# A decoder step on one core: another order of the steps in the front's projections and gates

## The reference, cut to what matters

```
xn   = rms_norm(x, g_attn)
proj = xn @ w_in      # columns: 512 pooling, 384 query latent, 256 kv latent, 32 rope, 2 x 1024 gates
q    = rms_norm(rope(rms_norm(q_lat) @ w_uq), head gains)     # 8 heads x 96
c_kv = rms_norm(c_kv);  k_r = rope(k_r)
k    = rms_norm([c_kv @ w_uk, k_r])                           # 8 heads x 96
d    = trailing means of u_pool over 2, 4, 8, 16 rows - u_pool
pool_out = (d @ w_pool_map) * pool_scale
gated    = (sigmoid(gate 0) * pool_out, sigmoid(gate 1))
```

## Time and profile before

| what | value |
|---|---|
| median of three runs | 2182.67 us (2181.5 to 2183.23) |
| profiled execution | 2183.03 us |
| its span | 2181.1 us |
| mean granted clock of TensorE | 0.979 |
| busy in the span | PE 2081.8, PEld 1915.4, DVE 1177.9, ACT 816.8, POOL 384.4 us |
| front ends on TensorE | 447.5 us; the attention's first product starts at 464.5 us |

### The profile page before, as it was taken

How to read it: one execution, slowest core, us unless ns; L and a number is a source line. 1 busy time by engine, 2 the same in 40 slices (tenths; PEclk the granted TensorE clock), 3 DMA queues, 4 the chain that set the end, 5 groups by cost and what they waited for, 6 DMA issues and landing times. The chain is left out here.

```text
span 2181.1 us, 35232 instructions
## 1 busy us (share of the span) xinstructions
PE 2081.8 (95%) x12669; PEld 1915.4 (88%) x12669; DVE 1177.9 (54%) x2356; ACT 816.8 (37%) x1589; POOL 384.4 (18%) x441
## 2 busy tenths in 40 slices
PE   6998999969988999999999989999999999999998
PEld 5887999968877999999999968899998989999997
DVE  3764311137765777677767744544444444444444
ACT  4553111136653566566656642422111112212111
POOL 1110000024441145355535420000000000000000
PEclk8999999989998999999999989999999999999999
DMA  4223222125422312222222134011111111111102
GB/s 153 86 74 96 60 80 80 66 80 152 127 73 64 88 36 64 72 67 66 63 71 66 34 119 175 22 57 58 39 58 38 38 38 40 57 38 58 38 19 87
DMA packets 146190, 152.69 MB, mean 70 GB/s; under 512 B 50694, under 2 KB 122102, under 8 KB 145021
## 3 DMA queue, kind: packets, MB, share of 16 engines
q1 hardware_dynamic: 140325, 128.28, 20.0%
q0 software_dynamic: 5728, 22.65, 3.3%
HBM read 124.77 MB, written 25.97 MB: 69 GB/s over the span
## 5 line engine op out<-in xcount | busy, mean ns | idle before, releaser
L104 PE MATMUL ps<-mh,f_w1h 128*128 128x384 f32 (+1 forms) x768 | 250.6, 326 | 0.0
L106 PE MATMUL ps<-mh,f_w1l 128*128 128x384 f32 (+1 forms) x768 | 250.5, 326 | 0.0
L105 PE MATMUL ps<-ml,f_w1h 128*128 128x384 f32 (+1 forms) x768 | 250.3, 326 | 0.0
L1920 ACT ACTIVATE tail_room<-ps 128x384 f32<-128x384 f32 (+1 forms) x96 | 45.5, 474 | 502.1 <-PE ps L106 502.1
L1373 ACT ACTIVATE sq<-ps 128x512 f32<-128x512 f32 x256 | 153.2, 598 | 207.6 <-PE ps L106 207.5
L1965 DVE TENSOR_TENSOR t_m<-t_m,ps 128x512 f32<-128x512 f32 x256 | 171.7, 685 | 106.9 <-PE ps L106 106.9
L105 PE MATMUL ps<-f_late_l,f_late_h 128*128 128x512 f32 x512 | 199.9, 390 | 0.0
L106 PE MATMUL ps<-f_late_h,f_late_l 128*128 128x512 f32 x512 | 199.8, 390 | 0.0
L104 PE MATMUL ps<-f_late_h 128*128 128x512 f32 x512 | 199.3, 389 | 0.0
L1945 DVE TENSOR_TENSOR tail_room<-tail_room 128x384 f32<-128x384 f32 (+1 forms) x96 | 51.5, 536 | 253.7 <-ACT tail_room L1920 253.7
L104 PE MATMUL ps<-wq,cTh 128*128 128x320 f32 x512 | 171.9, 336 | 2.4 <-DVE g_attn_b L1453 1.5
(11 more groups left out here) (350 smaller groups left out, 5045.9 us busy)
## 6 DMA issues: line engine op xcount, KB each, us to landing
f_raw<-in_w_ff SPq DMA_DIRECT2D x32, 1024.0 KB, 5.4
c_ring<-in_cache_kv_latent SPq DMA_DIRECT2D x192, 128.0 KB, 2.0
m_raw<-in_w_in SPq DMA_DIRECT2D x20, 512.0 KB, 3.9
gated<-gate POOLq DMA_DIRECT2D x8, 1088.0 KB, 5.1
pa_gm<-gated SPq DMA_DIRECT2D x16, 512.0 KB, 5.3
c_early<-in_cache_kv_latent SPq DMA_DIRECT2D x64, 128.0 KB, 2.1
fr_x<-in_x_prompt SPq DMA_DIRECT2D x8, 512.0 KB, 3.5
mixed<-pa_mixed SPq DMA_DIRECT2D x16, 256.0 KB, 2.2
```

The costliest lines, as they stand in the source:

```text
L104: nc.tensor.matmul(out, lh, rh, start=first, stop=False)
L105: nc.tensor.matmul(out, lh, rl, start=False, stop=False)
L106: return nc.tensor.matmul(out, ll, rh, start=False, stop=last)
L1920: nc.scalar.activation(z[:, a, 0:w], ps[:, 2 * par + a, 0:w], ACT.Relu).then_inc(S["relu"], 1)
```

## The change

The loop is taken apart into one function a step and engine, and these are called in a new order. No computation is added or dropped, and all instructions keep their shapes, but for where they stand and for the bank that one tile uses.

- Tile 1's latents go to banks 4 and 5 and follow tile 0's at once. The transposes of x of tile 1 stand between chunks 5 and 6 of tile 0's latents. For that SP loads x of tile 1 behind the fifth weight chunk and x of tile 2 ahead of `w_uq` and `w_uk`; ScalarE and VectorE handle x of tile 1 between weight chunks 4 and 5, and its high and low parts between chunks 6 and 7.
- Within a tile's latents all of bank 3 (288 columns) comes first, then the wait for `ctc`, then bank 2 (384 columns).
- ScalarE copies queries and keys of tile 7 inside step 8. The splits of chunks 0 to 3 are spread among the last tiles' steps.
- Heads of tile 7 follow project(0), heads of tile 8 follow project(1), the earlier state's transposes follow project(2), the tail's follow project(4).
- VectorE splits chunks 4 and 5 behind the first and second window, chunks 2 and 3 before all windows.
- The pooled products are issued as (j, 2), (j + 1, 0) after project(6 + 2j) and (j + 1, 1) after project(7 + 2j). VectorE splits chunk 7 + 2j before it scales (j, 2).

```diff
+        lat_bank = lambda i: 4 if i == 1 else 2
 # sync
-            for i, (pieces, *_rest) in enumerate(tiles):
-                wait_past(sp, s["xnd"], i - 1)
...
-                if i == 0:
-                    for k in range(KD):
...
+            load_x(0)
+            for k in range(KD):
+                wait_past(sp, wl_done, k - WR + 1)
+                sp.dma_start(wraw[k % WR], w_lat[:, k, :]).then_inc(w_in[k % WR], 16)
+                if k == WR - 1:
+                    load_x(1)
+            load_x(2)
+            sp.dma_start(w_uq[:], A["w_uq"].rearrange("(k p) n -> p k n", p=P)).then_inc(uq_in, 16)
+            sp.dma_start(w_uk, A["w_uk"].rearrange("(k p) h d -> p k (h d)", p=P)).then_inc(uq_in, 16)
+            for i in range(3, N):
+                load_x(i)
 # scalar
+            square_x(0)
+            copy_x(0)
+            for k in range(WR):
+                split_lat(k)
+            square_x(1)
+            split_lat(5)
+            split_lat(6)
+            copy_x(1)
+            split_lat(7)
+            copy_lat(0)
+            square_lat(0)
...
+            root_lat(0)
+            square_x(2)
+            copy_lat(1)
+            copy_turned(0)
+            copy_x(2)
+            square_lat(1)
+            root_lat(1)
+            copy_turned(1)
+            for g in range(2, N):
...
+                if g == N - 1:
+                    copy_qk(N - 2)
+                copy_q(g - 2, 1)
+            split_chunk(0)
+            square_qk(N - 2)
+            copy_qk(N - 1)
+            split_chunk(1)
+            square_qk(N - 1)
+            copy_q(N - 2, 0)
+            copy_q(N - 2, 1)
+            copy_channels(0)
+            split_chunk(2)
+            copy_q(N - 1, 0)
+            copy_q(N - 1, 1)
+            copy_channels(1)
+            split_chunk(3)
 # vector
+            mean_x(0)
+            scale_x(0)
+            low_x(0)
+            for k in range(WR):
+                low_lat(k)
+            mean_x(1)
+            scale_x(1)
+            low_lat(5)
+            low_lat(6)
+            low_x(1)
+            low_lat(7)
+            mean_lat(0)
+            scale_lat(0)
...
+            mean_x(2)
+            scale_x(2)
...
             dve.wait_ge(s["qkp"], N)
-            for c in range(2, 6):
-                split_chunk(c)
-                g = c - 2
+            for g in range(4):
...
+                if g < 2:
+                    split_chunk(4 + g)
                 for b, (lo, hi) in enumerate(groups):
                     i = 3 * j + b
+                    if b == 2 and 7 + 2 * j < NCH:
+                        split_chunk(7 + 2 * j)
...
-                if 7 + 2 * j < NCH:
-                    split_chunk(7 + 2 * j)
 # tensor
+            def latents(i):
+                pe.wait_ge(s["xtl"], 2 * i + 2)
+                if i >= 2:
+                    pe.wait_ge(s["latc"], 2 * i)
+                for k in range(KD):
+                    latent(i, k, 1)
+                if i >= 2:
+                    pe.wait_ge(s["ctc"], i)
+                for k in range(KD):
+                    last = latent(i, k, 0)
+                last.then_inc(s["latp"], 1)
+            turn_x(0)
+            pe.wait_ge(s["xtl"], 2)
+            for k in range(KD):
+                if k == 6:
+                    turn_x(1)
+                pe.wait_ge(wl_done, k + 1)
+                latent(0, k, 0)
+                last = latent(0, k, 1)
+            last.then_inc(s["latp"], 1)
+            latents(1)
+            turn_latents(0)
+            turn_x(2)
+            queries_and_keys(0)
+            turn_latents(1)
+            for g in range(2, N):
+                latents(g)
+                if g + 1 < N:
+                    turn_x(g + 1)
+                queries_and_keys(g - 1)
+                turn_heads(g - 2, 0)
+                turn_latents(g)
+                turn_heads(g - 2, 1)
+            queries_and_keys(N - 1)
+            project(0)
+            turn_heads(N - 2, 0)
+            turn_heads(N - 2, 1)
+            project(1)
+            turn_heads(N - 1, 0)
+            turn_heads(N - 1, 1)
+            project(2)
...
+            project(3)
+            project(4)
...
+            project(5)
...
-            for j in range(KD):
-                pooled(j)
-                if j + 1 < KD:
-                    project(6 + 2 * j)
-                    project(7 + 2 * j)
+            pooled(0, 0)
+            pooled(0, 1)
+            for j in range(KD - 1):
+                project(6 + 2 * j)
+                pooled(j, 2)
+                pooled(j + 1, 0)
+                project(7 + 2 * j)
+                pooled(j + 1, 1)
+            pooled(KD - 1, 2)
```

More of the change, by code:

```diff
@@ new lines, in copy_x, with split_lat @@
+            def copy_x(i):
+                r, x0 = tiles[i][1], tiles[i][3]
+                for half in range(2):
+                    act.wait_ge(s["xtp"], 2 * i + half + 1)
+                    nc.scalar.activation(xh[:, 4 * half:4 * half + 4, x0:x0 + r], four(ps[:, half, :], r),
+                                         ACT.Copy).then_inc(s["xth"], 1)
+            def split_lat(k):
+                act.wait_ge(w_in[k % WR], 16 * (k // WR + 1))
+                nc.scalar.activation(wlh[:, k, :], wraw[k % WR], ACT.Copy).then_inc(wh_done, 1)
@@ new lines, in root_lat, with copy_q @@
+            def root_lat(i):
+                r = tiles[i][1]
+                act.wait_ge(s["v2"], 2 * i + 2)
+                nc.scalar.activation(st[0:r, i, 7:9], st[0:r, i, 5:7], ACT.Sqrt).then_inc(s["s2"], 1)
+            def copy_q(i, half):
+                r = tiles[i][1]
+                act.wait_ge(s["qtp"], 2 * i + half + 1)
+                if not half:
+                    if i == 0:
+                        act.wait_ge(gains_done, 1)
+                        act.wait_ge(wl_done, KD)
+                    wait_past(act, qk_out[0], 16 * i)
+                nc.scalar.activation(out_qk[0:QK, 0, 4 * half:4 * half + 4, 0:r], four(ps[0:QK, 0, :], r),
+                                     ACT.Copy, scale=C["gqk"][:, 0:1]).then_inc(s["qtc"], 1)
@@ new lines, in sigmoid @@
+            def sigmoid(c):
+                bk, j, which = banks[c % 2], (c - 4) // 2, c % 2
+                act.wait_ge(M["proj"], c + 1)
+                if j >= 2:
+                    act.wait_ge(kept[j % 2], 16 * (j // 2))
+                if c == 4:
+                    act.wait_ge(qk_out[0], 16 * N)
+                    act.wait_ge(qk_out[1], 16 * N)
+                for b, (lo, hi) in enumerate(groups):
+                    ins = nc.scalar.activation(gate[:, j % 2, which, lo:hi], ps[:, bk[b], 0:hi - lo], ACT.Sigmoid)
+                ins.then_inc(M["sig"], 1)
@@ new lines, in mean_lat, with low_x @@
+            def mean_lat(i):
+                r = tiles[i][1]
+                dve.wait_ge(s["ss2"], 2 * i + 2)
+                nc.vector.tensor_scalar(st[0:r, i, 5:6], st[0:r, i, 3:4], 1.0 / QL, EPS, ALU.mult, ALU.add).then_inc(s["v2"], 1)
+                nc.vector.tensor_scalar(st[0:r, i, 6:7], st[0:r, i, 4:5], 1.0 / KV, EPS, ALU.mult, ALU.add).then_inc(s["v2"], 1)
+            def low_x(i):
+                r, x0 = tiles[i][1], tiles[i][3]
+                for half in range(2):
+                    dve.wait_ge(s["xth"], 2 * i + half + 1)
+                    nc.vector.tensor_tensor(xl[:, 4 * half:4 * half + 4, x0:x0 + r], four(ps[:, half, :], r),
+                                            f32(xh[:, 4 * half:4 * half + 4, x0:x0 + r]), ALU.subtract).then_inc(s["xtl"], 1)
@@ L544, in _, with copy_k @@
+            def copy_k(i, half):
+                r = tiles[i][1]
+                dve.wait_ge(s["ktp"], 2 * i + half + 1)
+                if not half:
                     if i == 0:
@@ L554, in _ @@
[L554 to L561 removed]
+                nc.vector.tensor_copy(out_qk[0:QK, 1, 4 * half:4 * half + 4, 0:r], four(ps[0:QK, 1, :], r)).then_inc(s["ktc"], 1)
@@ new lines, in queries_and_keys @@
+            def queries_and_keys(i):
+                r, c0 = tiles[i][1], tiles[i][4]
+                if i == 0:
+                    pe.wait_ge(uq_in, 32)
+                    pe.wait_ge(s["latc"], 4)
+                pe.wait_ge(s["qltc"], i + 1)
+                wait_past(pe, s["qkc"], 3 * i)
+                for half in range(2):
+                    for k in range(3):
+                        nc.tensor.matmul(ps[0:r, 4 + half, 0:4 * QK], qlT[:, k, 0:r],
+                                         w_uq[:, k, half * 4 * QK:(half + 1) * 4 * QK], start=k == 0, stop=k == 2)
+                pe.wait_ge(s["ctc"], i + 1)
+                if i == 0:
+                    pe.wait_ge(s["ukl"], 1)
+                for k in range(2):
+                    last = three_pass(nc, ps[0:r, 6, :], cTh[:, k, c0:c0 + r], cTl[:, k, c0:c0 + r],
+                                      w_ukh[:, k, :], w_ukl[:, k, :], k == 0, k == 1)
+                last.then_inc(s["qkp"], 1)
@@ new lines, in turn_latents @@
+            def turn_latents(i):
+                r = tiles[i][1]
```

(23 more changed lines are left out.)

535 lines of the change are left out of this document (217 added, 318 removed).

## The result

The changed kernel takes 2149.02 us (median, 2148.17 to 2149.71, four runs) against 2182.47 for the kernel before: 33.4 us less, a ratio of 0.9845 with a 95% interval of 0.9833 to 0.9858. The forecast was 2152.0 with a range of 2148 to 2159. The profiled execution took 2148.84 us, its span is 2146.9 us, and its mean granted clock 0.984 against 0.979.

The account below looks back on a forecast made before the run. TensorE's order was taken to set the front's length, with only its idle time and slow clock to win. Gains of 11.8 + 3.2 + 12.5 + 3.2 = 30.7 us gave 2152.0 us, range 2148 to 2159.

Parts of the forecast that it names:

- no hole in the start: First tiles: TensorE has no hole there, so more gain than forecast, 2147 to 2149.5 us; chance 0.05.
- First two tiles: Start of the front: new order takes back idle and cold time, gain 11.8 us, bounds 8 and 14.9.
- One bank ahead: Latents of the tiles: bank 3's products first cover the wait for turned latents, gain 3.2 us, bounds 2.2 and 3.6.
- Last tiles: Last tiles and first chunks: waits and slow clock go, gain 12.5 us, bounds 8 and 13.
- The cover to watch: VectorE's four windows move later; the last ends near 242.5 us where TensorE needs it near 250.
- the 4.3 of the step: Before tile 8's queries: copying tile 7's queries and keys earlier saves 2.45 us of wait and 1.8 us of slow clock.
- Pooled products: Gates: every product's bank is freed a projection earlier, gain 3.2 us, bounds 1.7 and 3.6.
- The clock: Rival, new start: the clock falls in holes of 0.6 and 1.8 us, 2153.8 to 2155.6 us; chance 0.17.
- The late x: Rival, start: tile 1's x lands at 16 to 17 us instead of 14.5, 2154 to 2156 us; chance 0.12.
- VectorE as the bound: Rival, last chunks: windows end 7.5 us later than counted, first pooled product waits, 2153 to 2158 us; chance 0.08.
- The slower rival: Gates: TensorE waits for VectorE's low parts at all 14 projections; at 3 us each 2194 us; chance 0.03.
- given back behind the front: Rival, behind the front: clock or transfers meeting other work return part of the gain, 2160 to 2172 us; chance 0.05.

Follow-up runs that it names:

- the late x: The changed kernel, but SP loads x of tile 1 behind the eighth weight chunk instead of the fifth: 2155.24 us (ratio 0.9875).
- VectorE's room: The changed kernel with unused extra additions on VectorE in the fourth window: 2155.82 us with eight, 2149.74 us with three.
- the last two tiles: The changed kernel, but ScalarE and VectorE split chunks 0 and 1 before the copy of tile 7's queries and keys: 2154.90 us (ratio 0.9871).
- bank: The kernel before with only bank 3's products ahead of the wait and bank 2's behind it: 2176.09 us (ratio 0.9977).

## Why the prediction was right

It held in range and direction, and all four terms came out at or above their size. The time itself is not where I had put most of my chances: 2149.02 us lies below my own forecast band (2149.5 to 2154.5), in the band of 2147 to 2149.5 to which I gave 0.05, and that band's reason, no hole in the start, did not hold. The traces won 34.2 us where 30.7 were forecast. Of the 3.5 us more, 1.8 are in the first two tiles, 1.0 in the three other parts, and 0.7 behind the front. Some 1.1 us of them (0.4 of the first load and those 0.7) are luck and not work of the change.

*First two tiles: the mis-sized term.* 11.8 us forecast, 13.6 measured, still within its bounds of 8 and 14.9. The holes were placed rightly (0.6 and 1.8 forecast, 0.56 and 1.43 measured), and so was the moment when x arrives. The term failed in its small parts, all counted too dear: the two holes are 0.4 us shorter in sum, the transposes of tile 2 start with no wait (0.5 us forecast), the turn of tile 0's latents takes 0.50 us (31.38 - 30.88) instead of 0.8, the other small waits (0.2) are absent, and the first load came 0.4 us sooner than in the profile before. No edit explains this last: in the traces of all kernels here the first instruction of TensorE stands between 7.96 and 8.54 us, and with the old start alone between 8.03 and 8.54. Together they make the 1.8 us.

*One bank ahead.* 3.2 us forecast, 3.76 measured, and 3.69 with that part alone. The step fell from 16.4 to 15.81 us: besides the idle 0.31 us the restart behind the wait went too. That the chains of ScalarE and VectorE might return a part as a wait did not occur; TensorE shows no idle time in that window.

*Last tiles.* 12.5 forecast, 12.8 measured. Every wait named went, 1.1 us stayed before tile 8's queries as computed. The cover to watch, VectorE's last window, was forecast 7.5 us ahead of need and is 7.1 us ahead; the room that counts is the 5.9 us behind the tail copies, which come after it. By the experiment that puts the two splits back, that one order is worth 5.2 us and not the 4.3 of the step, since its slow stretch can be longer; in the kernel before it was the shorter one.

*Pooled products.* 3.2 forecast, 3.33 measured. A pair of projections with its products takes 25.69 us; two projections and three products' content are 2 x 11.93 + 1.81 = 25.67. So the returns to a projection, for which the bounds ran from 0 to 0.27 us, cost about nothing.

*The rivals.* The clock did not fall in the new start: it is 1.00 from 20.40 to 38.05 us, across a hole of 1.43 us with eight transposes shortly before. What the Trainium skill says of transposes (TensorE: Matmul & The Clock Gate, Part 4: PE-mode transpose), that they don't count as busy, is not decided by this, since products stood around them. A stretch behind the front bears on it. There TensorE issues 16 transposes (L1707) behind a wait, and other products only from 652.28 us on; the clock is 0.50 from 649.30 us and 1.00 from 652.70:

```profile
649.00 3.34 PE L1707 MATMUL ps<-ident,prob 128*64 128x128 f32 x16 [4.58 <-PEq L926]
```

```profile
649.30:652.70 3.40, 3.40 (x19) 2.53 (x18) 2.78 (x6) 1.79 (x4) 3.26 (x2) 0.50 0.25 61
652.70:656.10 3.40, 2.67 (x31) 2.53 (x29) 3.34 (x6) 2.39 (x4) 1.03 (x3) 1.00 0.38 103
```

So here the clock came back behind transposes, and the weight that I gave this rival on their account has no support in the trace. The late x and VectorE as the bound did not happen, and the experiments show where each would have begun. The slower rival falls with the window of the gates, in which TensorE has no idle time at all. Nothing was given back behind the front; 0.7 us more was won there. It lies behind TensorE's wait for `f_raw`, which ends 832.9 us after the attention's first product in both traces: from there to the end of the span it took 883.7 us before and takes 883.0 us now. The slow stretch behind that wait was 11.47 us long and is 10.03 (first the window of before, then that of after):

```profile
1297.42:1308.89 11.47, 11.47 (x43) 10.50 (x44) 4.31 (x6) 5.46 (x7) 0.53 (x1) 0.50 1.03 373
1263.89:1273.92 10.03, 10.03 (x40) 9.35 (x41) 2.87 (x4) 4.38 (x6) 0.04 (x1) 0.50 1.07 379
```

At half speed 1.44 us less of it is worth 0.7 us. I take that for the cause; it was not tried by itself.

## What to carry to other kernels

When one engine is busy through nearly all of a stage, its idle time and its slow clock can be added up piece by piece from the trace, and orders that remove waits in different pieces add up too. Price a wait of 3.5 us or more on TensorE with what the clock takes behind it, here 1.7 to 2.8 us on top, as estimated from the experiments on the late x, on VectorE's room and on the last two tiles. To judge a part of 0.1 to 0.7%, cut the same piece of work out of both traces: it repeated within 0.1 us, where the medians of whole runs lay up to 2.5 us from it (bank: 6.2 against 3.7). Then look at the other pieces too, since a part can win something there.

## What the runs showed of the hardware

In the front, the granted clock fell to 0.50 in or just behind each of the waits of 3.55 to 6.28 us in these traces and behind none of 1.55 us or less. Of those between, the 3.02 us before the turn of tile 0's latents (32.02 in the kernel before) came when the clock was at 0.50 already. One behind the front, 2.84 us before transposes at 632.49 us in the changed kernel, also has a slow stretch, and so has its like in every kernel here:

```profile
632.49 1.09 PE L1211 MATMUL ps<-ident,pa_prob 128*128 128x128 f32 x4 [2.84 <-POOL pa_prob L1001]
```

```profile
632.20:635.60 3.40, 3.11 (x14) 2.93 (x15) 0.86 (x2) 0.77 (x2) 0.15 (x1) 0.50 0.17 66
```

At the very start the clock column is no measure: it shows 1.00 for 0 to 20.40 us after, yet the 384-column products at 11.84 to 13.84 us take 0.52 us each and those from 14.67 us on 0.34. How long the clock stays low after the same wait differs: behind 3.56 us before tile 8's queries, the twelve products took 5.80 us in one kernel and 6.80 us in another, with the same instructions. The wait of 0.31 us for another engine cost 0.59 us of a step, and that of 0.15 us before the third pooled product 0.42 us, so in these two places the idle time in the rows understates what a wait between matmuls costs by some 0.3 us.
